# Halving the work by tokens around the norms of a two-model kernel, with GpSimd summing the late squares

## The chip, the cores and the metric

One core of one Trainium2 chip. The metric is the device time of one execution, in microseconds (us). The kernel before takes 2888.39 us (median of 3 runs, 2888.19 to 2889.59).

## The reference

Two transformer blocks, each two layers deep, run one after the other in float32 on 512 tokens of width 1024. The first mixes by an mLSTM and a sliding window attention, the second by a pool, a neighbourhood attention and a retention; each layer then has a gated feed-forward with a short convolution (2816 wide). What matters here is what stands between the matrix products:

```python
for l in range(DEPTH):                       # first block
    h = rmsnorm(x, g_pre_mix[l])
    y = token_mixer(h, w_in[l], ..., w_out[l])
    x = x + rmsnorm(y, g_post_mix[l])
    h = rmsnorm(x, g_pre_ffn[l])
    y = conv_ffn(h, w_up[l], ffn_conv_w[l], w_down[l])
    x = x + rmsnorm(y, g_post_ffn[l])

def rmsnorm(x, g):
    y = x * rsqrt(mean(x * x, axis=-1) + EPS)
    return y * g
```

The second block adds 256 context tokens in its first layer (768 in all), norms before the mixer and before the feed-forward with a scale and a shift (`modulate`), adds the products to x through a gate, and ends with one more norm. A norm needs the mean over all 1024 features of a token, so nothing of it can be finished for a token before the last feature tile of the product ahead of it is there.

## The kernel before

**Layout.** Features lie on the 128 partitions, tokens along the free dimension; x is `X`, 8 chunks of 128 features. A product is a `Segment`: output tiles of 128 features, each summed over `kc` chunks (8, or 11 for the halves of the down projection). For each chunk three matmuls are made (`pe_chunk`, line 1012): high part of the weights by high and low part of the activations, low part of the weights by the high part. At 512 tokens each is one matmul of 512 columns; at 768 it is two of 384, into the two banks of one PSUM tile. There are six accumulators at 512 tokens and three at 768 (`columns`); PS[2] is kept for the norms.

**Weights.** SyncE loads a tile's weights into a ring of 6 or 4 slots when the slot's old tile is done (`load`). ScalarE copies them to the high part (`split_high`, line 842), VectorE subtracts for the low part (`split_low`, line 848). `Tile.splits` says behind which tile each split stands.

**A norm.** Each output tile is evicted by VectorE (`to_y` line 2250, `add_y` line 2253, or `gated_by` line 2288, which adds to X). ScalarE squares it into `SQ` (line 320), GpSimd adds the squares of tiles 0 to 6 into `SQSUM` (line 327), TensorE takes the mean over partitions by a matmul with `MEAN` of SQSUM and of the last square (lines 333, 336), and then runs 20 idle matmuls (line 259). ScalarE makes Ln and Exp of it (`Rstd`, lines 382, 384). Then a `Head` makes the next product's input, chunk by chunk:

- `GainHead` (behind the mixer and the feed-forward of the first block): VectorE scales Y (line 594), adds it to X (line 653), ScalarE makes the high part `HH` (line 634) and a square of X into Y (line 354), VectorE the low part `HL` (line 643). The order on VectorE is add(c), scale(c+1), low(c). The second norm is applied late: the product runs on unnormed x, VectorE adds the 8 squares by pairs (`HeadSquares.dve`, line 364) behind the head, TensorE makes the mean in the fourth tile, before its third chunk (line 368), and the outputs are multiplied by RSTD at eviction.
- `NormHead` (second block): VectorE makes T = X * scale * RSTD (line 719), ScalarE the high part with the shift (line 699), VectorE the low part (line 730). T has two buffers, and T(c) waits for low(c-2).
- `FinalHead`: 8 scalings of X (line 759) and 8 stores.

TensorE starts a new product with three tiles together (`together`): for each chunk, as its low part is ready, the matmuls of all three. At 768 tokens the third tile lags three chunks (`behind`), since its accumulator comes free later. All engines run their own list in order, and wait on counting semaphores; the order written in `tensor`, `scalar`, `vector` and `gpsimd` is the order of the run.

The norms concerned are those behind out1(0), ffn1(0), out1(1), out2(0), ffn2(0), out2(1) and ffn2(1); the one behind ffn1(1) stays as it was.

Of the kernel before, what the change touches and what calls it, by code (L numbers as in the profile page):

```python
# [7 lines left out]
F32 = mybir.dt.float32  # L8
# [5 lines left out]
P = 128  # L14
# [101 lines left out]
def build(nc, a, out):  # L116
    ctx = ExitStack()
    with ctx:
# [89 lines left out]
        class Segment:  # L208


            def __init__(self, weights, first, n, kc, hi, lo, tokens, kind="rows", out_act=None,
                         out_dve=None, squares=None, half=0, ready=None, together=1,
                         gh=None, gl=None, own=0, others=(), vec=None, tap_col=0, bias_col=None, late=False, mods=None, prep=None):
# [6 lines left out]
                self.mods, self.prep = mods, prep  # L220
# [23 lines left out]
        w_hi, w_lo, unit_done, acc_free = S("w_hi"), S("w_lo"), S("unit_done"), S("acc_free")  # L244
        own_done, tap_done, filtered = S("own_done"), S("tap_done"), S("filtered")
# [64 lines left out]
        class Squares:  # L310


            def __init__(self, run, n):
                self.n, self.done, self.added, self.summed = n, run.n_sq, run.n_added, run.n_summed
                run.n_sq, run.n_added, run.n_summed = run.n_sq + n, run.n_added + n - 2, run.n_summed + 1

            def act(self, act, c, src, tokens):
                if c > 1:
                    act.wait_ge(sq_added.sem, sq_added.at(self.added + max(1, c - 2)))
                act.activation(SQ[c % 2][:, 0:tokens], src, ACT.Square).then_inc(sq_done.sem, 1)  # L320

            def pool(self, pool, tokens):
                for c in range(1, self.n - 1):
                    pool.wait_ge(sq_done.sem, sq_done.at(self.done + c + 1))
                    if c > 1:
                        pool.wait_ge(sq_added.sem, sq_added.at(self.added + c - 1))
                    pool.tensor_tensor(SQSUM[:, 0:tokens], SQ[0][:, 0:tokens] if c == 1 else SQSUM[:, 0:tokens],  # L327
                                       SQ[c % 2][:, 0:tokens], ALU.add).then_inc(sq_added.sem, 1)

            def mean(self, pe, tokens):  # L330
                pe.wait_ge(sq_added.sem, sq_added.at(self.added + self.n - 2))
                for t0, tn in ranges(tokens):
                    pe.matmul(PS[2][:, t0:t0 + tn], MEAN[:], SQSUM[:, t0:t0 + tn], start=True, stop=False)
                pe.wait_ge(sq_done.sem, sq_done.at(self.done + self.n))
                for t0, tn in ranges(tokens):
                    ins = pe.matmul(PS[2][:, t0:t0 + tn], MEAN[:], SQ[(self.n - 1) % 2][:, t0:t0 + tn],  # L336
                                    start=False, stop=True)
                ins.then_inc(sq_summed.sem, 1)

            def wait_mean(self, act):  # L340
                act.wait_ge(sq_summed.sem, sq_summed.at(self.summed + 1))

        class HeadSquares:
# [5 lines left out]
            def __init__(self, run):  # L349
                self.done, self.added, self.summed = run.n_ysq, run.n_ysum, run.n_summed  # L350
                run.n_ysq, run.n_ysum, run.n_summed = run.n_ysq + DC, run.n_ysum + 7, run.n_summed + 1

            def act(self, act, c):
                act.activation(Y[:, c, :], X[:, c, 0:SEQ], ACT.Square).then_inc(ysq_done.sem, 1)
# [11 lines left out]
            def mean(self, pe):  # L366
                pe.wait_ge(ysq_added.sem, ysq_added.at(self.added + 7))
# [5 lines left out]
        class Rstd:  # L373


            def __init__(self, run, tokens):
                self.n, self.tokens = run.n_rstd, tokens
                run.n_rstd += 1

            def act(self, act):  # L380
                n = self.tokens
                act.activation(RSTD[:, 0:n], PS[2][:, 0:n], ACT.Ln, bias=EPSC[:, 0:1]).then_inc(log_done.sem, 1)  # L382
                act.wait_ge(log_done.sem, log_done.at(self.n + 1))
                act.activation(RSTD[:, 0:n], RSTD[:, 0:n], ACT.Exp, scale=-0.5).then_inc(rstd_done.sem, 1)  # L384

            def wait_log(self, eng):
                eng.wait_ge(log_done.sem, log_done.at(self.n + 1))

            def wait(self, eng):
                eng.wait_ge(rstd_done.sem, rstd_done.at(self.n + 1))  # L390

        class Head:
# [4 lines left out]
            def __init__(self, hi, lo, tokens):  # L397
                self.hi, self.lo, self.tokens = hi, lo, tokens
                self.late = None

            def plan(self, run):
                self.h0, self.before = run.n_h, run.squares
                run.n_h += DC

            def mark_hi(self, ins):
                ins.then_inc(h_hi.sem, 1)

            def wait_hi(self, dve, c):
                dve.wait_ge(h_hi.sem, h_hi.at(self.h0 + c + 1))

            def wait_lo(self, pe, c):
                pe.wait_ge(h_lo.sem, h_lo.at(self.h0 + c + 1))
# [180 lines left out]
        def scale_y(dve, gain, c):  # L593
            return dve.scalar_tensor_tensor(out=Y[:, c, :], in0=Y[:, c, :], scalar=gain(c), in1=RSTD[:, 0:SEQ],
                                            op0=ALU.mult, op1=ALU.mult).then_inc(y_scaled.sem, 1)

        class GainHead(Head):
# [12 lines left out]
            def plan(self, run):  # L610
                super().plan(run)
                self.y0 = run.n_y
                if self.gain:
                    run.n_y += DC
                    self.first = Rstd(run, SEQ)
                self.squares = HeadSquares(run)
                self.late = Rstd(run, SEQ)

            def act(self, act):
# [3 lines left out]
                else:  # L623
                    act.preload_act_table_set(LOG_EXP)
                    act.wait_ge(vec_in.sem, vec_in.at(16))
                    act.wait_ge(filled.sem, filled.at(5))
                for c in range(DC):
                    if self.gain:
                        act.wait_ge(added.sem, added.at(self.y0 + c + 1))
                    else:  # L630
                        if c in self.SPLIT_AT:
                            self.run.split_high(act, self.SPLIT_AT[c])
                        act.wait_ge(x_in[c].sem, x_in[c].at(16))
                    act.activation(self.hi[:, c, :], X[:, c, 0:SEQ], ACT.Identity, scale=self.scale(c),
                                   bias=ZERO[:, 0:1]).then_inc(h_hi.sem, 1)
                    self.squares.act(act, c)
                if not self.gain:
                    for u in range(4, self.run.ring):
                        self.run.split_high(act, u)

            def low(self, dve, c):
                self.wait_hi(dve, c)
                dve.scalar_tensor_tensor(out=self.lo[:, c, :], in0=X[:, c, 0:SEQ], scalar=self.scale(c),  # L643
                                         in1=self.hi[:, c, :].bitcast(F32), op0=ALU.mult,
                                         op1=ALU.subtract).then_inc(h_lo.sem, 1)

            def dve(self, dve):
                if self.gain:
                    self.first.wait(dve)
                    scale_y(dve, self.gain, 0)  # L650
                    for c in range(DC):
# [1905 lines left out]
```

## Time and profile before

| what | value |
|---|---|
| median of 3 runs | 2888.39 us |
| span of the profiled execution | 2888.5 us |
| TensorE busy, matmul | 2825.6 us, 98% |
| VectorE busy | 1762.3 us, 61% |
| ScalarE busy | 1128.9 us, 39% |
| GpSimd busy | 154.9 us, 5% |
| mean granted TensorE clock | 0.997 of full speed |

The page gives no time of the profiled execution besides its span, from the first to the last instruction; it lies within 0.2 us of the median. Matmuls overlap in the pipeline, so a matmul's listed duration (389 ns for 512 columns) is longer than the distance to the next one; the distance is what counts for the stream. The instructions of VectorE and ScalarE, too, start some 0.08 us before the one ahead of them is listed as ended.

### The profile page before, as it was taken

To read this page: it belongs to the slowest core of one execution; us is meant where nothing else is said; L and a number is where in the kernel's file an instruction comes from. 1 tells how busy PE (TensorE), PEld (TensorE's weight loads), DVE (VectorE), ACT (ScalarE), POOL (GpSimd) and SP (SyncE) were. 2 spreads that over 40 slices of the span, in tenths; PEclk is the share of its full clock that TensorE was granted. 3 is DMA by queue.
4 is the path that set the end of the run, shared out by engine and by line. 5 is a ranking of instruction groups with operands and counts; after the bars stand their busy time and mean duration, and the time that the engine had idled before them with its cause. 6 is when DMAs were issued, how large, how long until landed. Compare 5 with 4: busy or idle time off the path is not lost. (4 is left out here: it accounts for less than half of the span.)

```text
span 2888.5 us, 35552 instructions
## 1 busy us (share of the span) xinstructions
PE 2825.6 (98%) x14502; PEld 2383.8 (83%) x14502; DVE 1762.3 (61%) x2639; ACT 1128.9 (39%) x1684; POOL 154.9 (5%) x172
## 2 busy tenths in 40 slices
PE   9999999999999999999989999999999999999999
PEld 7657888878477888889956999999999975788887
DVE  6678766667668767766666565335534137664563
ACT  5255424443445424342255333223323236543342
POOL 0101000010110000100020100000000002100001
PEclk9999999999999999999999999999999999999999
DMA  5303243333122243435610112121121221232322
GB/s 207 110 16 117 91 143 102 90 129 117 52 81 81 94 140 102 119 108 204 234 48 30 59 66 66 56 69 66 62 61 62 66 96 53 75 102 85 112 84 84
DMA packets 84180, 269.93 MB, mean 93 GB/s; under 512 B 9265, under 2 KB 12209, under 8 KB 83633
## 3 DMA queue, kind: packets, MB, share of 16 engines
q1 hardware_dynamic: 84016, 267.66, 28.1%
q8 instruction: 115, 1.88, 0.3%
q14 instruction: 49, 0.39, 0.0%
HBM read 265.52 MB, written 2.10 MB: 93 GB/s over the span
## 5 line engine op out<-in xcount | busy, mean ns | idle before, releaser
L1012 PE MATMUL PS<-HH,WH 128*128 128x512 f32 (+1 forms) x3032 | 1001.0, 367 | 11.1 <-DVE WL L848 2.4
L1012 PE MATMUL PS<-HL,WH 128*128 128x512 f32 (+1 forms) x3032 | 992.0, 364 | 0.0
L1012 PE MATMUL PS<-HH,WL 128*128 128x512 f32 (+1 forms) x3032 | 991.8, 364 | 0.0
L848 DVE TENSOR_TENSOR WL<-STAGE,WH 128x1024 fp32r<-128x1024 f32 (+2 forms) x420 | 482.1, 1149 | 498.8 <-ACT WH L842 498.7
L842 ACT ACTIVATE WH<-STAGE 128x1024 fp32r<-128x1024 f32 (+2 forms) x420 | 407.4, 973 | 638.4 <-DMA STAGE<-in_w_down 275.1
L1012 PEld LDWEIGHTS PS<-HH,WH 128*128 128x128 f32 x3032 | 558.2, 188 | 92.0 <-DVE HL L643 10.7
L1012 PEld LDWEIGHTS PS<-HL,WH 128*128 128x128 f32 x3032 | 559.3, 188 | 64.5 <-issue 2.2
L1012 PEld LDWEIGHTS PS<-HH,WL 128*128 128x128 f32 x3032 | 559.3, 188 | 64.4
L1012 PE MATMUL PS<-GH,WL 128*128 128x512 f32 (+1 forms) x880 | 294.8, 367 | 0.0
L1012 PE MATMUL PS<-GL,WH 128*128 128x512 f32 (+1 forms) x880 | 294.8, 367 | 0.0
L1012 PE MATMUL PS<-GH,WH 128*128 128x512 f32 (+1 forms) x880 | 294.7, 367 | 0.0
L1012 PEld LDWEIGHTS PS<-GH,WH 128*128 128x128 f32 x880 | 162.7, 188 | 20.6
L1012 PEld LDWEIGHTS PS<-GL,WH 128*128 128x128 f32 x880 | 162.7, 188 | 20.5
L1012 PEld LDWEIGHTS PS<-GH,WL 128*128 128x128 f32 x880 | 162.6, 188 | 20.5
L983 DVE SCALAR_TENSOR_TENSOR CV<-PS,VEC,CV 128x384 f32<-128x384 f32 (+2 forms) x176 | 88.7, 546 | 93.5 <-ACT CV L938 92.0
L947 ACT ACTIVATE GH<-CV 128x512 fp32r<-128x512 f32 (+1 forms) x88 | 60.4, 686 | 190.4 <-DVE CV L992 190.4
L276 DVE SCALAR_TENSOR_TENSOR PS<-MODBUF,X 128x1024 f32<-128x1024 f32 x96 | 126.3, 1316 | 4.4
L983 DVE SCALAR_TENSOR_TENSOR CG<-PS,VEC,CG 128x384 f32<-128x384 f32 (+2 forms) x176 | 88.7, 546 | 54.5 <-ACT CG L938 52.9
L276 DVE SCALAR_TENSOR_TENSOR PS<-MODBUF,COND 128x1024 f32<-128x1024 f32 x64 | 78.9, 1233 | 52.0 <-DMA MODBUF<-in_w_mod 39.7
L969 DVE TENSOR_TENSOR U<-PS,RSTD 128x512 f32<-128x512 f32 x88 | 60.7, 690 | 79.8 <-PE PS L1012 74.2
L994 DVE TENSOR_TENSOR GL<-CV,GH 128x512 fp32r<-128x512 f32 (+1 forms) x88 | 66.8, 759 | 66.2 <-ACT GH L947 66.2
L327 POOL TENSOR_TENSOR SQSUM<-SQ,SQ 128x512 f32<-128x512 f32 (+1 forms) x8 | 12.5, 1556 | 1684.9 <-ACT SQ L320 1684.9
(231 smaller groups left out, 2459.5 us busy)
## 6 DMA issues: line engine op xcount, KB each, us to landing
STAGE<-in_w_up SPq DMA_DIRECT2D x176, 512.0 KB, 3.3
MODBUF<-in_w_mod SPq DMA_DIRECT2D x96, 512.0 KB, 4.2
STAGE<-in_w_in SPq DMA_DIRECT2D x84, 512.0 KB, 3.4
STAGE<-in_w_down SPq DMA_DIRECT2D x64, 384.0 KB, 3.1
STAGE<-in_w_down SPq DMA_DIRECT2D x64, 320.0 KB, 2.9
STAGE<-in_w_out SPq DMA_DIRECT2D x32, 512.0 KB, 4.4
BM<-in_na_bias SPq DMA_DIRECT2D x24, 256.0 KB, 2.6
CR<-in_const_ret SPq DMA_DIRECT2D x2, 1152.0 KB, 5.2
```

What stands on the lines that cost most here:

```text
L276: dve.scalar_tensor_tensor(out=PS[2][:].rearrange("p (c j) -> p c j", c=DC), in0=MODBUF[2 * self.l + buf][:], scalar=1.0, in1=cond, op0=AL ...
L327: pool.tensor_tensor(SQSUM[:, 0:tokens], SQ[0][:, 0:tokens] if c == 1 else SQSUM[:, 0:tokens], SQ[c % 2][:, 0:tokens], ALU.add).then_inc(s ...
L842: act.activation(WH[unit.slot][:, 0:size], STAGE[unit.slot][:, 0:size], ACT.Copy).then_inc(w_hi.sem, 1)
L848: dve.tensor_tensor(WL[unit.slot][:, 0:size], STAGE[unit.slot][:, 0:size], WH[unit.slot][:, 0:size].bitcast(F32), ALU.subtract).then_inc(w ...
L947: act.activation(seg.gh[:, t // 2, 0:n], CV[:, 0:n], ACT.Copy).then_inc(g_hi.sem, 1)
L969: dve.tensor_tensor(U[s][:, 0:n], self.whole(tile), RSTD[:, 0:n], ALU.mult).then_inc(acc_free.sem, 1)
L983: ins = dve.scalar_tensor_tensor(out=buf[:, a0 + shift:a0 + shift + an], in0=src[:, a0:a0 + an] if seg.late else self.acc(tile, col, an), ...
L994: dve.tensor_tensor(seg.gl[:, t // 2, 0:n], CV[:, 0:n], seg.gh[:, t // 2, 0:n].bitcast(F32), ALU.subtract).then_inc(g_lo.sem, 1)
L1012: ins = pe.matmul(self.acc(tile, col, tn), w[:, c:c + P], r[:, k, t0:t0 + tn], start=(k == 0 and m == 0), stop=(k == seg.kc - 1 and m == 2))
```

## The change

- The last tile of the product ahead of a norm is multiplied by halves of the tokens: all chunks for half 0, then all for half 1 (`pe_last`). At 512 tokens the halves are 256 columns in two accumulators; at 768 they are the two 384-column parts. Eviction and square come by halves (`half_evict`, `half_square`). The mean of half 0 stands in half 1, before its fourth chunk.
- Rstd and the head run for half 0, then for half 1 (`order`): 16 steps of half width instead of 8. Half 1 of the last tile is evicted and squared behind chunk 2 of half 0, its mean is made by TensorE behind chunk 2 of the first tiles, its Ln and Exp behind chunk 4 (`act_between`, `dve_between`).
- The first three tiles are multiplied for half 0, then for half 1 (`pe_first`); the third tile's lag of three chunks is there in half 0 only.
- The 20 idle matmuls go at these norms. Weight splits that stood behind the last tile are partly moved behind the head, or behind its chunk 1 where the first tiles need them (`early`).
- In GainHead with a gain the squares of X are summed by GpSimd, 7 adds in each half (`HeadSquares.pool`), no longer by VectorE.
- FinalHead scales and stores by halves, two chunks in a store.

```diff
+def halves_of(tokens):
+    return [(0, 0, SEQ // 2), (SEQ // 2, SEQ // 2, SEQ // 2)] if tokens == SEQ else parts_of(tokens)
...
 class HeadSquares:
+            def pool(self, pool):
+                for p, (_, t0, tn) in enumerate(self.parts):
+                    for c in range(1, DC):
+                        pool.wait_ge(ysq_done.sem, ysq_done.at(self.done + DC * p + c + 1))
+                        if c > 1:
+                            pool.wait_ge(ysq_added.sem, ysq_added.at(self.added + 7 * p + c - 1))
+                        pool.tensor_tensor(Y[:, 0, t0:t0 + tn], Y[:, 0, t0:t0 + tn], Y[:, c, t0:t0 + tn],
+                                           ALU.add).then_inc(ysq_added.sem, 1)
...
 class Head:
+            def act_between(self, act, rstd, p, c):
+                if not self.halved or p:
+                    return
+                last = self.before.seg.last()
+                if c == 1:
+                    for u in self.early:
+                        self.run.split_high(act, u)
+                if c == 2:
+                    self.run.half_square(act, last[-1], 1)
+                if c == 4:
+                    self.before.wait_mean(act, 1)
+                    rstd.act(act, 1)
...
+            def dve_between(self, dve, p, c):
...
+                if c == 1:
+                    for u in self.early:
+                        self.run.split_low(dve, u)
+                if c == 2:
+                    self.run.half_evict(dve, last[-1], 1)
...
 class GainHead:
+                    order = self.order()
+                    scaled(*order[0])
+                    for i, (p, c) in enumerate(order):
+                        _, t0, tn = self.parts[p]
+                        dve.wait_ge(y_scaled.sem, y_scaled.at(self.y0 + i + 1))
+                        dve.tensor_tensor(X[:, c, t0:t0 + tn], X[:, c, t0:t0 + tn], Y[:, c, t0:t0 + tn],
+                                          ALU.add).then_inc(added.sem, 1)
+                        if i + 1 < len(order):
+                            scaled(*order[i + 1])
+                        dve.wait_ge(added.sem, added.at(self.y0 + i + 1))
+                        self.low(dve, c, p)
+                        self.dve_between(dve, p, c)
...
 class FinalHead:
             def dve(self, dve):
                 self.norm.wait(dve)
+                for c in range(2):
+                    self.scaled(dve, c, 0)
+                self.run.half_evict(dve, self.before.seg.last()[0], 1)
+                for c in range(2, DC):
+                    self.scaled(dve, c, 0)
+                self.norm.wait(dve, 1)
                 for c in range(DC):
+                    self.scaled(dve, c, 1)
...
 class Run:
+            def pe_first(self, pe, head, seg):
+                first = seg.tiles[0:seg.together]
+                for p in range(2):
+                    behind = 3 if p == 0 and seg.tokens == TOK else 0
+                    for k in range(seg.kc):
+                        head.wait_lo(pe, k, p)
+                        for tile in first[0:2]:
+                            self.pe_chunk(pe, tile, k, p)
+                        for tile in first[2:]:
+                            if k >= behind:
+                                self.pe_chunk(pe, tile, k - behind, p)
+                        if p == 0 and k == 2:
+                            head.before.mean(pe, 1)
+                    for k in range(seg.kc - behind, seg.kc):
+                        for tile in first[2:]:
+                            self.pe_chunk(pe, tile, k, p)
...
+            def pe_last(self, pe, seg):
+                last = seg.last()
+                for tile in last:
+                    for k in range(seg.kc):
+                        self.pe_chunk(pe, tile, k, 0)
+                for tile in last:
+                    for k in range(seg.kc):
+                        if tile is last[0] and k == 3:
+                            seg.sums.mean(pe, 0)
+                        self.pe_chunk(pe, tile, k, 1)
...
-                        if seg.squares:
-                            seg.sums.mean(pe, seg.tokens)
+                        if seg.halved:
+                            self.pe_last(pe, seg)
+                        elif seg.squares:
+                            seg.sums.mean(pe)
                             idle(pe, 20, 3)
```

## Rows read from the trace of the kernel before

**Rows 1.** The page's part 1: busy us, share of the span, instructions.
```profile
PE 2825.6 (98%) x14502; PEld 2383.8 (83%) x14502; DVE 1762.3 (61%) x2639; ACT 1128.9 (39%) x1684; POOL 154.9 (5%) x172
```
**Rows 2.** The chain that ended last: start us, us, what.
```profile
2517.30 359.11 PE PS L1012 x1584
```
**Rows 3.** Line 1012 by stretch, B1 to B6: us, busy (matmuls), clock, DMA, GB/s.
```profile
240.21:274.46 34.25, 25.47 (x103) 1.00 0.24 84
608.79:646.50 37.71, 27.50 (x112) 1.00 0.26 89
857.88:892.34 34.46, 25.71 (x103) 1.00 0.24 85
1630.70:1673.90 43.20, 34.02 (x193) 1.00 0.15 49
2186.66:2233.10 46.44, 37.13 (x211) 1.00 0.18 57
2504.59:2533.50 28.91, 22.06 (x97) 1.00 0.14 39
```
**Rows 4.** The same of a stretch with 384-column matmuls only.
```profile
2245.00:2300.00 55.00, 55.00 (x319) 1.00 0.18 58
```
**Rows 5.** Timeline of the first norm (ScalarE, VectorE, TensorE): start us, us, instruction.
```profile
247.67 0.69 ACT L382 ACTIVATE RSTD<-PS,EPSC 128x512 f32<-128x512 f32 x1 [0.27 <-PE PS L336]
...
250.56 0.81 ACT L634 ACTIVATE HH<-X,ZERO,VEC 128x512 fp32r<-128x512 f32 x1 [1.55 <-DVE X L653]
251.28 0.61 ACT L354 ACTIVATE Y<-X 128x512 f32<-128x512 f32 x1
...
249.05 0.75 DVE L594 SCALAR_TENSOR_TENSOR Y<-Y,VEC,RSTD 128x512 f32<-128x512 f32 x1 [0.40 <-ACT RSTD L384]
...
251.48 0.75 DVE L643 SCALAR_TENSOR_TENSOR HL<-X,VEC,HH 128x512 fp32r<-128x512 f32 x1 [0.29 <-ACT HH L634]
252.15 0.68 DVE L653 TENSOR_TENSOR X<-X,Y 128x512 f32<-128x512 f32 x1
...
252.28 0.50 PE L1012 MATMUL PS<-HH,WH 128*128 128x512 f32 x1 [0.19 <-DVE HL L643]
```
**Rows 6.** Groups by shape: count, busy us, mean ns, idle before.
```profile
L730 DVE SCALAR_TENSOR_TENSOR HL<-T,MOD,HH 128x256 fp32r<-128x256 f32 x24 | 11.5, 480 | 0.0
...
L699 ACT ACTIVATE HH<-T,MOD 128x512 fp32r<-128x512 f32 x32 | 23.1, 725 | 29.8 <-DVE T L719 29.8
L699 ACT ACTIVATE HH<-T,MOD 128x256 fp32r<-128x256 f32 x24 | 11.9, 494 | 0.0
...
L327 POOL TENSOR_TENSOR SQSUM<-SQSUM,SQ 128x768 f32<-128x768 f32 x10 | 18.5, 1845 | 69.2 <-ACT SQ L320 69.2
```
**Rows 7.** Timeline: GpSimd's adds, and VectorE beside them and alone.
```profile
240.20 1.55 POOL L327 TENSOR_TENSOR SQSUM<-SQSUM,SQ 128x512 f32<-128x512 f32 x1 [2.43 <-ACT SQ L320]
244.17 1.29 POOL L327 TENSOR_TENSOR SQSUM<-SQSUM,SQ 128x512 f32<-128x512 f32 x1 [2.43 <-ACT SQ L320]
...
241.11 1.72 DVE L848 TENSOR_TENSOR WL<-STAGE,WH 128x1024 fp32r<-128x1024 f32 x1 [0.45 <-ACT WH L842]
...
247.43 1.23 DVE L848 TENSOR_TENSOR WL<-STAGE,WH 128x1024 fp32r<-128x1024 f32 x1 [0.25 <-ACT WH L842]
...
1466.89 0.88 DVE L2144 TENSOR_SCALAR PN<-PN,SM 128x512 f32<-128x512 f32 x2
...
1481.44 1.24 DVE L2144 TENSOR_SCALAR PN<-PN,SM 128x512 f32<-128x512 f32 x2
...
1481.68 0.72 POOL L1884 TENSOR_TENSOR KD<-KR,SM 128x256 f32<-128x256 f32 x1 [3.45 <-ACT SM L2078]
```
**Rows 8.** Timeline of ScalarE and VectorE behind B4's first tile.
```profile
1668.94 0.99 ACT L938 ACTIVATE CG<-PS,VEC 128x768 f32<-128x768 f32 x1 [6.12 <-PE PS L1012]
...
1669.97 2.57 DVE L983 SCALAR_TENSOR_TENSOR CG<-PS,VEC,CG 128x384 f32<-128x384 f32 x6 [5.78 <-ACT CG L938]
```
**Rows 9.** Timeline of VectorE in the tail.
```profile
2880.44 5.39 DVE L759 SCALAR_TENSOR_TENSOR X<-X,FIN,RSTD 128x512 f32<-128x512 f32 x8 [3.26 <-ACT RSTD L384]
```

More of the change, by code:

```diff
@@ L322, in pool @@
-            def pool(self, pool, tokens):
+                act.activation(SQ[c % 2][:, t0:t0 + tn], src, ACT.Square).then_inc(sq_done.sem, 1)
+            def pool(self, pool):
                 for c in range(1, self.n - 1):
[L324 to L336, printed above, removed]
+                    for p, (_, t0, tn) in enumerate([(0, 0, self.tokens)] if c < self.whole else self.parts):
+                        pool.wait_ge(sq_done.sem, self.squared(c, p))
+                        if c > 1:
+                            pool.wait_ge(sq_added.sem, self.sums(c - 1))
+                        first = SQ[0] if c == 1 else SQSUM
+                        pool.tensor_tensor(SQSUM[:, t0:t0 + tn], first[:, t0:t0 + tn], SQ[c % 2][:, t0:t0 + tn],
+                                           ALU.add).then_inc(sq_added.sem, 1)
@@ new lines, in mean @@
+            def mean(self, pe, p=0):
+                runs = [(SEQ * p, *self.parts[p][1:])] if self.halved else [(t0, t0, tn) for t0, tn in ranges(self.tokens)]
+                pe.wait_ge(sq_added.sem, self.sums(self.n - 2, p))
+                for col, t0, tn in runs:
+                    pe.matmul(PS[2][:, col:col + tn], MEAN[:], SQSUM[:, t0:t0 + tn], start=True, stop=False)
+                pe.wait_ge(sq_done.sem, self.squared(self.n - 1, p))
+                for col, t0, tn in runs:
+                    ins = pe.matmul(PS[2][:, col:col + tn], MEAN[:], SQ[(self.n - 1) % 2][:, t0:t0 + tn],
@@ L637, in act @@
[L637 to L644, printed above, removed]
+                    for p, c in self.order():
+                        act.wait_ge(added.sem, added.at(self.y0 + self.nth(p, c) + 1))
+                        self.high(act, p, c)
+                        self.act_between(act, self.first, p, c)
@@ L675, in plan @@
                 self.t0, self.y0, self.x0 = run.n_t, run.n_y, run.n_x
-                run.n_t += DC
+                run.n_t += DC * len(self.parts)
                 if self.gain:
@@ L749, in plan @@
             def plan(self, run):
-                self.before, self.norm = run.squares, Rstd(run, SEQ)
+                self.before = run.squares
+                self.halved, self.parts = True, self.before.parts
+                self.norm = Rstd(run, SEQ, self.parts)
             def act(self, act):
@@ L808, in __init__ @@
                             tiles.append(tile)
+                        for tile in seg.last() if seg.halved else ():
+                            tile.half, self.n_half = self.n_half, self.n_half + 1
                     if segments:
@@ L817, in __init__ @@
                 assert u == len(self.units), (u, len(self.units))
+                for (_, ending), (head, beginning) in zip(parts, parts[1:]):
+                    if not ending[-1].halved or not beginning:
+                        continue
+                    held, first = ending[-1].last(), beginning[0].tiles[0]
+                    until = held[0].units[0].u + ring
+                    put_off = [u for tile in held for u in tile.splits if u >= until] + first.splits
+                    for tile in held:
+                        tile.splits = [u for u in tile.splits if u < until]
+                    begun = beginning[0].tiles[0:beginning[0].together]
+                    head.early = [u for u in put_off if self.units[u].tile in begun]
+                    first.splits = put_off[len(head.early):]
                 self.mod_loads = {}
@@ L1111, in gpsimd @@
                         if seg.squares:
[L1112 removed]
+                            seg.sums.pool(pool)
         def stream(run, mixer=None):
```

346 lines of the change are left out of this document (225 added, 121 removed).

## The prediction

> **What bounds the kernel now.** First the page's busy shares: TensorE is busy 98% of the span, VectorE 61%, GpSimd 5% [rows 1]. Then the chain that ended last: nearly all of it is long stretches of line 1012, as the 1584 matmuls in 359.11 us [rows 2], 0.2267 us per matmul of 512 columns. So TensorE's stream sets the time, and what can be won is where it stops. Third, the stretches around the norms, each from the first matmul of the last tile to the first matmul behind the norm's work (in the three with a late mean that one is the seventh of the fourth tile, otherwise the fourth tile's first) [rows 3]. Call them B1 to B6. Needed there are 102, 111, 102, 192, 210 and 96 matmuls; at 0.2267 us, or at 0.1724 us (55/319 [rows 4]; 0.173 below) for the 384-column ones of B4 and B5, the stretches hold 11.1, 12.5, 11.3, 9.9, 10.0 and 7.1 us that are not product matmuls, 62 us in all. The seventh is the tail behind the last matmul, some 12 us, with the final scaling in it [rows 9]. The granted clock is 1.00, that is 2.4 GHz, in all of them, so no clock is to be won.
>
> The first norm in detail [rows 5]: Ln starts at 247.67, the first scaling at 249.05, the first product at 252.28. From there each chunk runs VectorE's add (252.15), ScalarE's high part (0.72 us after the add starts), VectorE's low part (0.92 us after the high part starts), then the next add 0.67 us after: 2.31 us, where TensorE needs 9 x 0.2267 = 2.04. The chain of latencies, not VectorE's busy time, paces the first three tiles.
>
> **Halving the matmuls.** No 256-column product is in the trace. 512 columns take 226.7 ns and 384 take 172.4 to 173.3: the slope is 0.416 ns a column, so 256 come to 0.120 us [rows 2, 4]. Bounds: 0.113 (half of 512) and 0.173 (as 384, were a floor in the weight load). I take 0.120, the line through both. Where tokens are 768, halves are the same two 384-column parts in another order: nothing is added. At 512 tokens, 24 or 33 matmuls of the last tile and 72 of the first three double: half 0 of a last tile takes 2.9 us (4.0 with 33 matmuls).
>
> *TensorE: Matmul & The Clock Gate*, section "Back-to-back issue gap", of the Trainium skill gives N/2.4 + 2.5 ns alone, 109 ns at 256 columns, and warns that the weight load can set the pace of small ones. The trace's 226.7 ns at 512 is above its 216; by its figure the PE-bound B6 would be about 2 us shorter, with the estimate from that page.
>
> **Halving the element work.** STT 0.75 to 0.48, the high part's slope is 0.23 us for 256 columns (0.725 to 0.494), so 0.81 becomes 0.59; the add falls by the same slope as STT from 0.68 to 0.42, Ln and Exp by 0.21 each, a square from 0.61 to 0.40 [rows 5, 6]. GpSimd's add: 512 in 1.29, 768 in 1.85, so 256 in 0.73 [rows 6, 7], and the measured 256-column add is 0.72.
>
> **B1 (post-mix norm, layer 0).** The last tile begins at 240.22. Half 0 is out at 243.1, TensorE goes on into half 1 and reaches the mean nine matmuls later, 244.2. It must wait there: tile 6's square is late (its sum begins at 244.17 [rows 7]), the half sum ends at 244.9. Mean 0.87, Ln at 246.05, scaling 0.95 later at 247.0 (half of the 1.38 from 247.67 to 249.05 that is width), low part 1.67 later at 248.7, product 249.2: three us earlier than 252.28. Half 1 covers most of this gap; the twenty idle matmuls that go cost nothing.
>
> But then each half chunk repeats the whole latency chain: add 0.42+0.04, high part 0.59+0.10, low part to next add 0.40 = 1.55 us, against 1.15 for half of the old one. TensorE needs 9 x 0.12 = 1.08. Fifteen steps make 23.2 us.
>
> Into this goes GpSimd's sum of squares, 7 adds in each half. An add of GpSimd and an instruction of VectorE that reads two SBUF operands keep each other out: the weight split takes 1.23 alone and 1.72 when it starts while GpSimd adds, and ends 1.08 after GpSimd does; GpSimd's add takes 1.55 instead of 1.29 when VectorE was first [rows 7]. All three VectorE steps of the chain read two SBUF operands. Counted from the high part's start, the square is ready and GpSimd starts at 0.98, the low part holds VectorE until 1.17, and the next add would start at 1.09. Who gets in? The trace has this geometry once: VectorE's two scalings started 0.40 apart take 0.88; with a GpSimd add begun between their starts they take 1.24, so the second was held back and GpSimd went first, its 0.72 hardly longer [rows 7]. So I take it that GpSimd goes first: it ends at 1.17+0.59, the add ends 0.28 later at 2.04 instead of 1.51, and a step costs 0.5 more. Adds 1 to 7 each hold back one step of the next, 6+1+6 = 13 (the late eviction between is hidden there): 6.5 us. Bounds: 0 (no hold) and 0.59 a step, 7.7 us. 0.5 stands nearest to the row.
>
> *SBUF — State Buffer*, section "Who interferes with whom", of the Trainium skill says the same as a lock: two SBUF inputs against a GpSimd instruction that reads SBUF, and whoever issues first holds the pair for the whole instruction. The trace agrees, 1.72 against 1.23. It doesn't say who wins between two queued VectorE instructions.
>
> Last low part at 248.7+23.2+6.5 = 278.4, product 0.53 later, nine matmuls 1.08: three tiles done at 280.0 (270.6 before). The late mean then finds its sum ready; before, TensorE stood 1.6 us for VectorE's seven adds. So the stretch ends at 280.0 + 6 x 0.2267 + 0.87 = 282.2: 42.0 us for 34.25, **+7.7**.
>
> **B2** has an adding eviction and 33 matmuls a half, so more time in half 1: scaling at 616.15, held by the weight split on VectorE, last low part 31.4 later (1.67+23.2+6.5), stretch 42.6 for 37.7, **+4.9**. **B3** is B1 again (ring of 4): the fourth tile's weight split, which VectorE does behind the norm, costs a wait of 1.0 (before 1.5): 43.0 for 34.5, **+8.5**.
>
> **B4 and B5 (768 tokens).** No extra matmuls and no GpSimd sum in the chain. B4: half 0 at 1634.7, mean at 1636.4 to 1637.7, Ln and Exp 1.15, first product at 1641.05 instead of 1648.37; second mean and late eviction cost about 0.9 near k = 3; three tiles done at 1667.85 instead of 1673.9. The low parts then keep ahead (1.2 and 1.4 a chunk against 1.56). But in half 1 the third tile no longer lags three chunks, so all three end together, and with three accumulators the fourth tile waits for the first one's eviction: 0.4 + ScalarE 0.99 + VectorE 2.57 [rows 8] after a tile that ends 1.2 before: 2.85 us. Net **-3.2**. B5 has a short eviction there (0.2), but the third tile's weights are split inside the norm, their slot comes free only in half 1: 2.3 us of waiting at k = 2. 41.7 for 46.4: **-4.7**.
>
> **B6** (512 tokens, scaled norm): a half step is 0.91 us, T 0.40 and low part 0.51 after one another, under TensorE's 1.08. First product at 2512.55 for 2517.05, then 144 x 0.12 + 0.87 + 0.2 = 18.35: **-2.6**.
>
> **Tail.** Mean at 2873.8 inside half 1, half 0 scaled mostly before the second half is evicted at 2878.2, six scalings 2.4, eight more at 0.40: last scaling ends 2883.85, before 2885.83 (eight in 5.39 from 2880.44 [rows 9]). Store and end as before: **-2.0**.
>
> Sum: +7.7+4.9+8.5-3.2-4.7-2.6-2.0 = **+8.6**. The profiled span is 2888.5, the median 2888.4, so I predict **2897 us**, slower by 0.30%.
>
> **Rivals.**
> (a) GpSimd never holds the chain back. Against: 1.72 and 1.24 [rows 7]; for: none of VectorE's steps in this chain was ever seen beside GpSimd. Without the 6.5 us, but with 1.25 for the late eviction and second Ln that then show, three times: 15.8 less, 2881, **faster**. It decides at a hold below 0.2 us a step.
> (b) VectorE's add wins the race by being queued, GpSimd goes between add and next scaling: a step costs 0.12, 1.5 us a norm instead of 6.5, and part of the 1.25 shows: 2885, no change to speak of.
> (c) 256-column matmuls run at 0.173. The GpSimd-paced norms hide most of it (9 x 0.173 = 1.56 under 2.05), B6 does not: +8.9 there, some 7 elsewhere: 2913.
> (d) Halves don't reach what they are for: the pause at the norms stays, since ScalarE or VectorE is busy with a weight split when half 0 is out. B2's and B6's scalings are held 0.2 already; 1 us at each of seven places gives 2904.
>
> **Numbers.** Forecast with GpSimd first, (d) in small amounts within: 0.60. (a) 0.18, (b) 0.15, (c) 0.04, (d) in full 0.03. The likeliest one's own range is 2891 to 2903. For 8 in 10 I need (b) and half of (a): 2880 to 2903. A difference under 0.2%, 5.8 us (2882.6 to 2894.2), is no change that a measurement tells: slower 0.47, within 0.32, faster 0.21.
>
> **What would show it.** In the profile after: the norm with gains steps at about 2.05 us per 256-column half chunk, VectorE's add of X and Y near 0.9 instead of 0.42; GpSimd's Y sums 0.73 to 0.8; the product 0.120 apart; TensorE's gap before the first product near 3 us or less, no wait at the late mean; a wait of 2.8 us on the eviction at B4's fourth tile. Wrong if the add stays at 0.42 (then (a)), if the scaling is the long one (then (b)), or if the product spacing is above 0.13.

## The result, and the profile after

The changed kernel takes **2903.06 us** (median of 4, 2901.25 to 2906.32), the kernel before 2888.57 in the same job: ratio 1.0048, 95% interval 1.0034 to 1.0063, 14.5 us slower. Forecast were 2897 us and 8.6 us. The direction and nearly every mechanism were right; some 6 us are missing, and the median lies on the upper edge of the stated range, 2880 to 2903. The profiled execution spans 2902.2 us, 13.7 more than before. An execution's listed time is 1.7 to 1.8 us longer than its span, so the profiled execution of the kernel before (span 2888.5) must have taken some 2890.2 us, 1.6 to 1.8 above its median, and not within 0.2 us of it; 13.7 is the difference of two single executions, 14.5 that of the medians.

First the same stretches as [rows 3], now of line 1195 of the changed kernel: start:end, length, TensorE busy (matmuls), weight loads busy, granted clock, DMA share, GB/s. The last row lies between B4 and B5.

```profile
239.75:282.64 42.89, 31.89 (x199) 27.66 (x198) 0.92 0.14 49
616.93:661.60 44.67, 33.62 (x217) 29.71 (x216) 0.92 0.21 70
871.69:915.66 43.97, 30.50 (x200) 26.30 (x198) 0.96 0.15 50
1652.32:1692.17 39.85, 34.77 (x193) 33.00 (x193) 0.99 0.15 50
2206.38:2249.48 43.10, 38.50 (x212) 36.70 (x211) 0.96 0.12 38
2522.72:2548.96 26.24, 24.01 (x194) 23.40 (x193) 1.00 0.12 41
1692.16:2206.37 514.21, 514.20 (x2958) 514.20 (x2959) 1.00 0.20 63
```

The forecast's terms beside it. "Again" is a second profiled execution of the same kernel (e12), "filled" is e9, in which the clock did not fall in these stretches:

| us against before | forecast | after | again | filled |
|---|---|---|---|---|
| B1 | +7.7 | +8.6 | +8.8 | +8.9 |
| B2 | +4.9 | +7.0 | +5.3 | +5.3 |
| B3 | +8.5 | +9.5 | +10.5 | +9.5 |
| B4 | -3.2 | -3.4 | -3.3 | -3.3 |
| between B4 and B5 | 0 | +1.5 | +1.6 | +0.1 |
| B5 | -4.7 | -3.3 | -4.9 | -5.1 |
| B6 | -2.6 | -2.7 | -2.6 | -2.3 |
| behind B6, with the tail | -2.0 | -1.8 | -1.8 | -1.8 |

(B1 is 42.89 - 34.25, and so on. What is left of the 13.7 us, -1.7, lies in the other stretches, mostly the attention; more of them under e12.)

What the forecast did not have is the clock column: 0.92, 0.92, 0.96, 0.99, 0.96, where [rows 3] has 1.00 six times. The mean of the whole execution says the same, first the kernel before, then the changed one (span, mean granted clock):

```profile
core 0: 2888.5 us, clock 0.997
```

```profile
core 0: 2902.2 us, clock 0.993
```

At 1.2 instead of 2.4 GHz the clock lacks a half, so 0.003 x 2888.5 / 0.5 = 17 us were spent at 1.2 GHz before, and 0.007 x 2902.2 / 0.5, some 40 us, after. By fine windows over both traces these are pieces of 3.4 us, called falls here: five before, ten after, and after also the last 5.5 us, in which TensorE has no more work. Seven of the ten lie in B1 to B5 and between B4 and B5, where before there was none. Two places by finer stretches of the changed kernel, all engines (the order is PE, PEld, DVE, ACT, POOL, then clock, DMA, GB/s): the end of B2, and B4's fourth tile.

```profile
655.00:658.50 3.50, 2.73 (x17) 2.53 (x18) 2.06 (x3) 2.69 (x4) 1.28 (x2) 0.86 0.00 0
658.50:661.50 3.00, 3.00 (x10) 2.31 (x9) 1.55 (x2) 0.11 (x1) 0.00 (x0) 0.60 0.93 329
...
1690.00:1692.20 2.20, 0.03 (x1) 0.03 (x1) 2.08 (x6) 0.40 (x1) 0.00 (x0) 0.90 0.98 378
1692.20:1695.60 3.40, 3.40 (x12) 3.40 (x13) 2.68 (x5) 3.37 (x4) 0.00 (x0) 0.56 0.54 190
1695.60:1700.00 4.40, 4.40 (x27) 4.40 (x26) 3.38 (x6) 2.52 (x4) 0.00 (x0) 1.00 0.00 0
```

In each pair TensorE first works with pauses or stands (2.73 of 3.5 us busy, 0.03 of 2.2), then it is fully busy at a clock of 0.60 and 0.56. In 3.4 us it makes 12 matmuls, in the next 4.4 it makes 27. (The fall of the second pair begins in the wait, at 1691.7.)

Now the loop of the norms with gains, two half chunks of B1 in the changed kernel's timeline (start us, us, instruction; TensorE's lines left out):

```profile
258.47 0.40 ACT L384 ACTIVATE Y<-X 128x256 f32<-128x256 f32 x1
258.67 0.48 DVE L724 SCALAR_TENSOR_TENSOR HL<-X,VEC,HH 128x256 fp32r<-128x256 f32 x1 [0.34 <-ACT HH L697]
258.95 0.79 POOL L392 TENSOR_TENSOR Y<-Y 128x256 f32<-128x256 f32 x1 [1.30 <-ACT Y L384]
259.07 0.96 DVE L740 TENSOR_TENSOR X<-X,Y 128x256 f32<-128x256 f32 x1
...
259.95 0.47 DVE L670 SCALAR_TENSOR_TENSOR Y<-Y,VEC,RSTD 128x256 f32<-128x256 f32 x1
...
260.06 0.60 ACT L697 ACTIVATE HH<-X,ZERO,VEC 128x256 fp32r<-128x256 f32 x1 [1.19 <-DVE X L740]
...
260.77 0.48 DVE L724 SCALAR_TENSOR_TENSOR HL<-X,VEC,HH 128x256 fp32r<-128x256 f32 x1 [0.34 <-ACT HH L697]
261.05 0.79 POOL L392 TENSOR_TENSOR Y<-Y 128x256 f32<-128x256 f32 x1 [1.30 <-ACT Y L384]
261.17 0.95 DVE L740 TENSOR_TENSOR X<-X,Y 128x256 f32<-128x256 f32 x1
```

This is the forecast's picture to the tenth. GpSimd starts while VectorE's low part runs (258.95 in 258.67 to 259.15), is there ahead of VectorE's next add, and the add takes 0.96 instead of 0.42 us. Step: 260.77 - 258.67 = 2.10 us. Of B1's 15 steps 13 take 2.10 and two 1.56. In 12 of the 13 VectorE's add takes 0.95 or 0.96 us; the other one has the late eviction in it, and takes 2.00 without GpSimd too (e2).

### The profile page after: what moved, and what is told of

Its sections match the earlier page's. It is cut to its first block and busy times, and to the rows that moved or that the text cites. A ratio compares the mean times of both kernels' runs of the same rounds, so it can differ in the third digit from the quotient of the medians.

```text
span 2902.2 us, 36228 instructions
## 1 busy us (share of the span) xinstructions
PE 2810.6 (97%) x14668; PEld 2391.6 (82%) x14668; DVE 1790.4 (62%) x2751; ACT 1150.1 (40%) x1777; POOL 188.3 (6%) x214
## 5 line engine op out<-in xcount | busy, mean ns | idle before, releaser
L1195 PE MATMUL PS<-HH,WH 128*128 128x512 f32 (+2 forms) x3152 | 1038.9, 362 | 40.6 <-DVE HL L724 28.2
L1195 PE MATMUL PS<-HL,WH 128*128 128x512 f32 (+2 forms) x3152 | 1025.2, 358 | 0.0
L1195 PE MATMUL PS<-HH,WL 128*128 128x512 f32 (+2 forms) x3152 | 1024.8, 358 | 0.0
L1195 PEld LDWEIGHTS PS<-HH,WH 128*128 128x128 f32 x3152 | 586.0, 189 | 119.5 <-DVE HL L724 38.4
L1195 PEld LDWEIGHTS PS<-HL,WH 128*128 128x128 f32 x3152 | 587.0, 189 | 61.4 <-issue 2.5
L1195 PEld LDWEIGHTS PS<-HH,WL 128*128 128x128 f32 x3152 | 586.7, 189 | 59.3
L1195 PE MATMUL PS<-GH,WH 128*128 128x512 f32 (+2 forms) x902 | 301.0, 363 | 0.0
L1195 PE MATMUL PS<-GH,WL 128*128 128x512 f32 (+2 forms) x902 | 300.4, 362 | 0.0
L1195 PE MATMUL PS<-GL,WH 128*128 128x512 f32 (+2 forms) x902 | 300.3, 362 | 0.0
L287 DVE SCALAR_TENSOR_TENSOR PS<-MODBUF,COND 128x1024 f32<-128x1024 f32 x64 | 78.9, 1233 | 52.6 <-DMA MODBUF<-in_w_mod 39.9
```

The source lines that it names most:

```text
L287: dve.scalar_tensor_tensor(out=PS[2][:].rearrange("p (c j) -> p c j", c=DC), in0=MODBUF[2 * self.l + buf][:], scalar=1.0, in1=cond, op0=AL ...
L1195: ins = pe.matmul(self.acc(tile, col, tn, p), w[:, c:c + P], r[:, k, t0:t0 + tn], start=(k == 0 and m == 0), stop=(k == seg.kc - 1 and m = ...
```

## The experiments

Ratios are against the kernel before, run in the same job; its median moves from 2887.5 to 2889.3 us between jobs. "B1 to B6" are the stretches above. The edits are given in short form, against the changed kernel where nothing else is said.

**e1, norms with gains whole again.**

```diff
-  out1:    halved=1
-  ffn1(0): halved=1
+  not halved; GainHead.pool only where halved
```

> The changed kernel, but the three norms with gains (B1, B2, B3) whole as before, only the four scaled norms (B4, B5, B6, tail) halved. Theory (GpSimd's adds hold VectorE in the halved norms with gains; these three stretches lost 8.6 + 7.0 + 9.5 = 25.1 us, the four others won 3.3 + 3.35 + 2.7 + 1.8, less 1.5 for the half clock behind B4): B1 to B3 return to 34.3, 37.7 and 34.5 us, and the time is 2888.5 - 9.7 = 2879, faster than before by 0.33%. Rival (halving as such costs, and the norms with gains are only where it shows): the four scaled norms win nothing net, 2888 or more.

Measured 2879.57 us, ratio 0.9966 (0.9954 to 0.9979): faster by 0.34%, the forecast to half a microsecond. B1 to B3 take 34.26, 37.72 and 34.28 us, B4 39.86, B5 42.94, B6 26.48. In the four scaled norms halving wins: the loss lies in the three norms with gains. Whether halving or GpSimd's sum makes it there, this run can't tell (e2 can).

**e2, VectorE sums the squares.**

```diff
-  GainHead.pool: 7 adds of 256 columns in each half (GpSimd)
+  vector(): seven adds of 512 columns behind the norm, as before
```

> The changed kernel, but in the halved norms with gains VectorE adds the squares behind the norm, seven whole adds, as before the change; GpSimd does nothing there. Theory (hold): VectorE's add of X and Y takes 0.42 instead of 0.95 us, a step 1.55 instead of 2.10, 13 steps x 0.54 = 7.0 us less a norm; the late eviction and second Ln then show, 1.25, and TensorE waits 2.3 us again at the late mean (B3 0.6): some 14 us less in all, 2889 +- 3. Rival (the step of 2.10 is the small instructions' own chain, GpSimd is innocent): the step stays 2.10, seven adds of 0.68 come on top, 2908.

2896.87 us, ratio 1.0027 (1.0017 to 1.0037). The step is what the hold theory says: two of VectorE's low parts in e2's timeline are 260.12 - 258.55 = 1.57 us apart, and the add is back at 0.42.

```profile
258.55 0.48 DVE L724 SCALAR_TENSOR_TENSOR HL<-X,VEC,HH 128x256 fp32r<-128x256 f32 x1 [0.34 <-ACT HH L697]
258.96 0.42 DVE L740 TENSOR_TENSOR X<-X,Y 128x256 f32<-128x256 f32 x1
259.29 0.48 DVE L670 SCALAR_TENSOR_TENSOR Y<-Y,VEC,RSTD 128x256 f32<-128x256 f32 x1
260.12 0.48 DVE L724 SCALAR_TENSOR_TENSOR HL<-X,VEC,HH 128x256 fp32r<-128x256 f32 x1 [0.34 <-ACT HH L697]
```

The total I had expected was 8 us too low, because of what stands behind the loop:

```profile
273.00 2.49 DVE L403 TENSOR_TENSOR Y<-Y 128x512 f32<-128x512 f32 x4
275.40 1.22 DVE L991 TENSOR_TENSOR WL<-STAGE,WH 128x1024 fp32r<-128x1024 f32 x1
276.54 2.01 DVE L403 TENSOR_TENSOR Y<-Y 128x512 f32<-128x512 f32 x3
```

From the last low part (272.60) to the end of B1 (279.17) it is 6.6 us; in the changed kernel, where GpSimd sums meanwhile, 3.6 (279.08 to 282.64). B1 to B3 come to 39.86, 40.83 and 40.38. The loop's 15 steps take 23.88 us here (248.72 to 272.60) and 30.35 in the changed kernel, so in B1 GpSimd's sum costs 6.5 us and gives 3.0 back. e2 also shows what halving alone does to these norms: +5.6, +3.1, +5.9 (with the clock at 0.98 and 0.97 in B2 and B3). The first low part comes 9.41 instead of 11.27 us after the last tile's start (B2: 8.83 instead of 14.72), but from the first low part to the last, 16 halves take 23.9 us and 8 wholes 16.1, 7 x 2.31.

**e3, TensorE sums the squares.**

```diff
+  for each half chunk, in pe_first:
+      matmul(PS[2][:, t0:t0+256], MEAN, Y[:, c, half], start=(c==0), stop=(c==7))
-  all adds of Y squares, the late mean
```

> The changed kernel, but in the halved norms with gains nobody adds the squares: TensorE multiplies each chunk's squares by the mean matrix and accumulates (16 matmuls of 256 columns in fp32, 0.215 us each, inside the loop; the late mean of 0.43 goes). Theory (hold): step 1.55, TensorE needs 9 x 0.120 + 0.215 = 1.30 of it, so each norm is 7.0 - 1.25 + 0.43 = 6.2 us shorter, and the busier TensorE keeps its clock, which gives back some 2 us: 2882 +- 3. Rival (the clock falls all the same): at 1.2 GHz a step is 9 x 0.213 + 0.43 = 2.35, in phases of some 3.4 us, and TensorE becomes the bound there: 2887 or more.

2879.95 us, ratio 0.9970 (0.9959 to 0.9981). Step 1.56, no fall of the clock in B1 to B3 (start:end, length, busy (matmuls), loads, clock):

```profile
238.74:275.14 36.40, 29.51 (x199) 25.57 (x198) 1.00 0.16 55
609.02:645.59 36.57, 31.48 (x217) 27.54 (x216) 1.00 0.22 69
856.54:893.44 36.90, 29.44 (x200) 25.53 (x199) 1.00 0.17 59
```

Against the changed kernel -6.5, -8.1 and -7.1 us. I had a price wrong: a matmul of fp32 operands shows as two records, so a chunk's mean takes 2 x 0.215 = 0.43, and TensorE needs 1.08 + 0.43 = 1.51 of 1.56 us, which just fits. B2 is now 1.1 us shorter than before the change, B1 and B3 still 2.2 and 2.4 longer.

**e4, unread matmuls where TensorE stands.**

```diff
+  fill(pe, 6)  behind each half chunk of the norms with gains
+  fill(pe, 20) in B5 ahead of k = 2
+  fill(pe, 24) ahead of the fourth tile at 768 tokens
```

> The changed kernel with matmuls that nobody reads where TensorE stands: six of 128 columns behind each half chunk of the norms with gains (0.66 us of the 1.0 that it waits), 20 in B5 ahead of k = 2, 24 ahead of B4's fourth tile. Theory (the falls of the granted clock cost what was missed: B2 1.2, B3 0.9, behind B4 1.5, in B5 1.2): the clock is 1.00 throughout, every wait and the step of 2.10 stay as long, and the time is 4.8 us less, 2898. Rival (the clock falls only where TensorE waits anyway and costs nothing): 2903, no change.

2927.59 us, ratio 1.0133 (1.0119 to 1.0147): the filling was too long. Each of these fp32 matmuls is two records of 0.111 us as well, so six took 1.33 us, TensorE's step became 9 x 0.12 + 1.33 = 2.4, and B1 49.8 us. The clock did stay up in B1 and behind B4, and between B4 and B5 it is 512.8 us. Nothing on the price of a fall follows from the total.

**e5, GpSimd's adds half as wide.**

```diff
-  pool.tensor_tensor(Y[:, 0, 256 columns], ...)
+  pool.tensor_tensor(Y[:, 0, 128 columns], ...)      (the sum of the other 128 is left out)
```

> The changed kernel, but each of GpSimd's adds in the norms with gains covers 128 of the 256 columns (the other half of the sum is left out). Theory (VectorE's add is held until GpSimd's add ends, and starts 0.28 us before nothing else): GpSimd's add takes some 0.45 instead of 0.79 us, so VectorE's add of X and Y takes 0.6 instead of 0.95, the step is 1.75 instead of 2.10, and 13 steps in each of three norms give 13.6 us back: 2889. Rival (a hold costs the same whatever the length of GpSimd's add, as if by its semaphores or a fixed change of owner): step 2.10, 2903.

2894.21 us, ratio 1.0014 (1.0005 to 1.0023). In e5's timeline GpSimd's add takes 0.52, VectorE's 0.68, and the held steps are 1.82:

```profile
265.73 0.52 POOL L393 TENSOR_TENSOR Y<-Y 128x128 f32<-128x128 f32 x1 [2.86 <-ACT Y L384]
...
265.85 0.68 DVE L741 TENSOR_TENSOR X<-X,Y 128x256 f32<-128x256 f32 x1
```

GpSimd's add became 0.27 shorter, and VectorE's 0.28. So the hold follows the length of GpSimd's add; a fixed price is ruled out. My 0.45 for the 128-column add was too low, which is the difference to 1.75. The total is 5 us above the 2889 expected: B1 is 39.55, 3.3 us less than in the changed kernel, where 13 steps of 0.35 would have been 4.6.

**e6, half the filling.**

```diff
-  fill 6 / 20 / 24
+  fill 3 / 9 / 12
```

> The changed kernel with half the unread matmuls of e4: three behind each half chunk of the norms with gains (each is two passes of 0.111 us, so 0.67 of the 1.0 us that TensorE waits), 9 in B5, 12 ahead of B4's fourth tile. Theory (clock falls cost what was missed): the steps stay 2.10, B4 39.85, no fall of the clock in B1 to B5 and behind B4: B2 -1.2, B3 -0.9, behind B4 -1.5, B5 -1.4 us, 2898. Rival (the falls cost nothing, TensorE waits there anyway): 2903.

2901.37 us, ratio 1.0043 (1.0030 to 1.0056). The steps stay 2.10, B2 is 43.0 and the part between B4 and B5 512.9, but B5 takes 43.8: the 12 matmuls stood ahead of its fourth tile too, where nothing waited. So e9 repeats it without those.

**e7, the third tile's lag in half 1.**

```diff
-  behind = 3 if p == 0 and seg.tokens == TOK else 0
+  behind = 3 if seg.tokens == TOK else 0
```

> The changed kernel, but the third tile of a 768-token segment lags three chunks in half 1 too. Theory (B4's fourth tile waits 2.8 us for the eviction of the first tile, since all three end together): three chunks of the third tile, 9 x 0.173 = 1.56 us, now lie over the eviction, the wait is 1.25 us, B4 38.3; the clock behind it may then not fall (-1.5): 2900 to 2901.5. Rival (the wait is for something else, VectorE or the weights of the fourth tile): it stays 2.8 us behind the third tile's end, and the time 2903.

2899.70 us, ratio 1.0037 (1.0024 to 1.0050). B4 and what follows it:

```profile
1651.23:1689.52 38.29, 34.77 (x194) 33.01 (x193) 1.00 0.14 48
1689.51:2202.36 512.85, 512.84 (x2958) 512.84 (x2959) 1.00 0.20 64
```

B4 is 1.56 us shorter than after (39.85), which is 9 x 0.173, and with a wait of 1.25 instead of 2.81 us the clock didn't fall behind it: 512.85 for 514.21. A wait for the fourth tile's weights or for VectorE would have stayed as long behind the third tile's end; this one was for the first tile's eviction.

**e8, the parts that pay together.**

```diff
   B1, B3: whole, as e1;  B2: halved, sums by TensorE, as e3
   scaled norms: halved, lag in half 1, as e7
+  fill(pe, 9) in B5, fill(pe, 5) ahead of the fourth tile at 768 tokens
```

> B1 and B3 whole as before the change; B2 halved with its squares summed by TensorE inside the loop; the scaled norms halved as in the changed kernel, with the third tile's lag in half 1; unread matmuls where TensorE stands in B5 (9) and at B4's fourth tile (5). Theory: 2879.6 of the kernel with whole norms with gains, B2 -1.2, B4 -1.6, no half clock behind it -1.5, nor in B5 -1.4: 2874, faster than before by 0.5% and than that kernel by 0.2%. Rival (the falls move elsewhere instead of going): 2877 or more.

**2871.74 us**, ratio 0.9937 (0.9925 to 0.9950): faster than both kernels, 17 us under the one before, and 2.3 us under what I had added up for it. Its profiled execution has two falls of the clock ahead of its last matmul, where the kernel before has five.

**e9, e6 with the filling in its place.**

```diff
-  fill(pe, 12) ahead of B4's and B5's fourth tile
+  fill(pe, 12) ahead of B4's only
```

> e6 with its 12 unread matmuls only ahead of B4's fourth tile; e6 had them ahead of B5's fourth tile too, where nothing waited, and its trace shows a pause of 2.6 us there. Theory (clock falls cost what was missed): 2901.4 - 2.6 = 2898.8, B2 43.0, B5 41.2 and 512.9 us between B4 and B5. Rival (the falls only move to other places, so that filling gains nothing): 2901 or more.

2901.66 us, ratio 1.0046 (1.0033 to 1.0058). B2, B5 and between B4 and B5:

```profile
615.97:658.99 43.02, 31.14 (x218) 27.20 (x216) 1.00 0.17 60
...
2205.43:2246.79 41.36, 37.61 (x212) 36.24 (x211) 1.00 0.12 40
1692.60:2205.42 512.82, 512.82 (x2958) 512.82 (x2959) 1.00 0.20 63
```

In place the theory holds: 1.65, 1.74 and 1.39 us less than after, 4.8 together, with the steps of the loops still 2.10. But the total did not gain: 14.2 us above the kernel before in the same job, for 14.5, and no less than e6. The rival has the total. In this execution the stretches from B2 to B3 and from B3 to B4, with the attention in them, are 1.3 and 1.8 us longer than in the changed kernel's.

**e10, e8 with less filling.**

```diff
-  fill(pe, 5) ahead of B4's and B5's fourth tile
+  fill(pe, 5) ahead of B4's only
```

> e8 without the five unread matmuls ahead of B5's fourth tile (1.03 us of pause in e8's trace). Theory: 2871.7 - 1.0 = 2870.7, faster than before by 0.6%. Rival (without them the clock falls in or behind B5): 2872 to 2873.

2872.18 us, ratio 0.9944 (0.9930 to 0.9957), no better than e8. B5 did come down, from 42.27 to 41.34, but 1.6 us came back in the attention behind it. Nearly the same work there, first in e8, then in e10 (all engines, then clock, DMA, GB/s):

```profile
2366.00:2370.00 4.00, 2.02 (x17) 1.40 (x15) 3.97 (x7) 2.67 (x7) 0.00 (x0) 1.00 0.20 66
2370.00:2374.00 4.00, 3.55 (x17) 1.99 (x18) 3.93 (x9) 2.60 (x6) 2.54 (x2) 1.00 0.18 66
```

```profile
2366.00:2370.00 4.00, 2.07 (x9) 1.32 (x10) 3.96 (x9) 3.57 (x8) 0.00 (x0) 0.78 0.22 66
2370.00:2374.00 4.00, 3.75 (x14) 1.88 (x14) 3.97 (x7) 1.06 (x3) 2.19 (x2) 0.79 0.18 66
```

The rival of this run held for the time. One execution of each doesn't show that the five matmuls decide whether the clock falls there: e12 shows falls that differ between two executions of one kernel.

**e11, GpSimd's sum alone, norms with gains whole.**

```diff
   as e1, and
-  VectorE's seven adds behind the norm
+  GpSimd's add of 512 columns behind each square
```

> The kernel of e1 (norms with gains whole), but GpSimd sums the late squares there, one whole add of 512 columns behind each square, instead of VectorE's seven behind the norm: the last part of the change alone. Theory (hold, from the length of GpSimd's add): an add of 512 columns takes 1.29 to 1.35 us and holds VectorE's next add until it ends, so a step is some 2.31 + 1.1 = 3.4 us on six of seven steps, +6.5 us in each of B1 to B3, and TensorE's wait at the late mean goes, -2.3, -2.3 and -0.6: 2879.6 + 14 = 2894. Rival (the hold is peculiar to the short steps of the halves; with whole chunks GpSimd fits into the 0.29 us that VectorE is idle and costs nothing): step 2.31, the wait at the late mean gone, 2874.5.

2892.38 us, ratio 1.0010 (1.0001 to 1.0019), 12.8 us slower than e1 (13.5 if each is taken against its own job's kernel before). The step is 3.40 us, as expected; one of them in e11's timeline:

```profile
261.27 1.40 POOL L392 TENSOR_TENSOR Y<-Y 128x512 f32<-128x512 f32 x1 [2.00 <-ACT Y L384]
...
261.45 1.78 DVE L740 TENSOR_TENSOR X<-X,Y 128x512 f32<-128x512 f32 x1
```

VectorE's add takes 1.78 instead of 0.68 [rows 5]. B1 to B3 are 38.78, 42.23 and 39.04, some +4.5 each against before. So the fault of the sum is not one of halves: it costs with whole chunks too, in a loop in which VectorE's queued add of two SBUF operands paces TensorE.

**e12, the changed kernel again.**

> The changed kernel once more, for a second profiled execution. Theory (a fall of the clock in the halved norms follows from TensorE's waits there, one in the attention is set by how the execution happens to lie): B1 to B6 take the same time within 0.3 us, with half clock at the end of B2 and B3, behind B4 and in B5; the stretches between them, with the attention in it, differ by up to 1.8 us each from the first execution. Rival (all falls lie as they happen): B2, B3, behind B4 or B5 differ by over 1 us from the first execution.

2904.51 us, ratio 1.0054 (1.0042 to 1.0067). B1, B4 and B6 agree within 0.2 us. B2, B3 and B5 do not: -1.6, +1.0 and -1.6, with clocks of 0.96, 0.92 and 1.00 for 0.92, 0.96 and 0.96. B1 has two falls in both executions, and the stretch behind B4 has its one in both. So I was wrong that all falls in the halved norms are fixed by the kernel: those in B2, B3 and B5 are not. In the whole execution there are eleven for ten.

The stretches between, with the attention in them, do the same work in all these kernels. Their lengths in us, with the number of falls in each:

| | before | after | again | filled (e9) |
|---|---|---|---|---|
| B2 to B3 | 211.4 (2) | 210.1 (1) | 211.4 (2) | 211.4 (2) |
| B3 to B4 | 738.4 (1) | 736.7 (0) | 736.7 (0) | 738.4 (1) |
| B5 to B6 | 271.5 (0) | 273.2 (1) | 273.2 (1) | 273.2 (1) |

One fall more or less is the whole difference in each row: 1.3, 1.7 and 1.7 us. (B5 to B6 is 271.6 in e8, without a fall, and 273.2 in e10, with one.)

## Why the prediction was right, and where it was short

**The hold** was right in place, order and price: GpSimd goes between the low part and the add, and costs the loop 30.35 - 23.88 = 6.5 us, as forecast, 12 adds of 0.54 instead of 13 steps of 0.50. What was short is the loop without it: 23.88 us instead of 23.2, because the late eviction was put at nothing ("hidden there") and its step takes 2.00 us for 1.56 (e2). So the 15 steps take 30.35 us (248.73 to 279.08) instead of 29.7, 0.65 more in each of three norms. Rival (a), no hold, and (b), VectorE's add first, are refuted by the timeline above and by e2 and e5; (d) is out in B1, where TensorE's pause ahead of the first product is 1.6 us. The Trainium skill, *SBUF — State Buffer*, section "Who interferes with whom", has it that the port pair shared by VectorE and GpSimd is an exclusive lock, and that issue order decides who blocks; e5 and e11 agree, since VectorE's add, begun second, ends 0.29 us (e5: 0.28, e11: 0.56) after GpSimd's, whether that takes 0.52, 0.79 or 1.40 us.

**Start of the loop.** B1's mean comes 5.17 us after the last tile's start (4.68 in the forecast). GpSimd's add of tile 6's square is still whole in the changed kernel, 1.27 us for 512 columns, where the forecast put half of it, 0.73. With the 0.65 this makes up B1's and B3's +0.9 to +1.0. The first product comes 3.0 us earlier than before in time of the clock (249.27 for 252.28), 2.6 counted from the tile's start; at the late mean TensorE doesn't wait, as written.

**Matmuls of 256 columns** start 0.120 us apart where the clock is up, the value taken; rival (c) is out. B6 is within 0.1 us, the tail within 0.3.

**B4** is within 0.2 us, with a wait of 2.81 us (2.85 forecast), and e7 shows its cause. **B5** has its wait at k = 2 (2.15, forecast 2.3) and, without a fall, -4.9 to -5.1.

**The clock is what failed.** The prediction said that the granted clock is 1.00 in all stretches, "so no clock is to be won", and stopped there: it asked what could be won, not what could be lost. It put the 20 idle matmuls that go at nothing (their share was not run by itself), and did not ask what the clock does in loops in which TensorE works 1.08 of 2.10 us, where before it worked 2.04 of 2.31. How much each part made of the miss, by the profiled executions: e9, in which no fall is left in B1 to B6, has +11.3 us by its column, so 2.7 of the miss are sizes, most of them the two above. The changed kernel spans 2.3 us more than e9: its falls in B2, in B5 and behind B4 cost 4.8, and two falls fewer in the attention give 3.0 back, with small differences in the rest. The clock's 4.8 us are thus shown place by place, but in the total 3.0 of them are won back in the attention, which fits that the filling didn't pay. The medians are 14.5, 15.9 (e12) and 14.2 us (e9) above the kernel before. That what they have beyond 11.3 is all clock is likely but not shown: single executions of one kernel lie 3 to 5 us apart. Nothing in the range was there for falls of the clock; that the median still lies at its edge is luck.

**The two halves of the change** part cleanly. Scaled norms and tail halved: -9.8 us (e1, 2879.57 for 2889.34). Norms with gains, lengths of B1, B2, B3:

| | whole | halved |
|---|---|---|
| VectorE sums behind the norm | 34.3, 37.7, 34.3 | 39.9, 40.8, 40.4 |
| GpSimd sums in the loop | 38.8, 42.2, 39.0 | 43.2, 43.0, 44.0 (e9, without falls) |
| TensorE sums in the loop | not run | 36.4, 36.6, 36.9 |

In this chain of latencies each half costs more than half (1.56 for 2.31). The only halved norm with a gain that came out shorter than before is B2 with TensorE's sums, by 1.1 us; there halving brought the first low part forward the most (14.7 to 8.8 us). As TensorE's sums with whole chunks were not run, what halving and what the sum has of that is open.

## What to carry to other kernels

Before a piece of work moves to GpSimd, look at which of VectorE's instructions lie beside it and whether they are on a chain that TensorE waits for: an add that is "free" there can hold each of them for most of its own length (VectorE's add of 0.42 us took 0.96 beside one of 0.79). Halve a step only where its engine is the bound or TensorE's gap ahead of it is longer than the added latencies, here 15 x 1.56 against 7 x 2.31 us. And when TensorE gets pauses inside a loop, budget for its clock: in a trace look at the clock column of the stretch behind a pause, count the falls of the whole execution, and expect a repair to move a fall as easily as to remove it.

## What the runs showed of the hardware

- The clock's falls are pieces of 3.4 us at 1.2 GHz. One costs 1.4 us between B4 and B5 (514.21 for 512.82) and 1.7 in B5 (43.10 for 41.36), where TensorE is the bound, and nothing in a loop that VectorE paces (B1 is 42.9 with a clock of 0.92, 43.2 with 1.00 in e9).
- One can come without a long stand of TensorE. Ahead of B1's first fall in the changed kernel it was busy 2.65 of 4.3 us, with 1.6 us as its longest stand (the first row; the fall is the second):

```profile
247.00:251.30 4.30, 2.65 (x20) 2.24 (x20) 3.53 (x8) 1.83 (x5) 0.73 (x1) 1.00 0.37 122
251.30:254.70 3.40, 3.20 (x16) 2.91 (x15) 2.69 (x7) 2.08 (x5) 0.85 (x2) 0.50 0.00 0
```

- Some falls come in one execution of a kernel and not in the next (B2, B3 and B5 in after and e12), and the kernel before has them in its attention too, which fits its spread of 2885.0 to 2892.1 us in the later jobs.
- A matmul of fp32 operands shows as two records: 2 x 0.215 us at 256 columns, 2 x 0.111 at 128.
- GpSimd's add takes 0.52 us at 128 columns, 0.79 at 256 and 1.40 at 512, beside VectorE.
